# Moving x's split halves and the mixers' outputs by 32 bytes in a four-layer decoder on one Trainium2 core

## The reference

```python
for i in range(DEPTH):                      # DEPTH = 4
    mixer = i % 3
    h = rmsnorm(x, norm_mix[i])
    if mixer == 0:
        y = hgrn2_mixer(h, a_w_in[j], lower_bounds[j], a_head_norm[j], a_w_out[j])
    elif mixer == 1:
        y = moba_mixer(h, b_w_qkv[j], b_w_out[j], rel_bias)
    else:
        y = pool_mixer(h, c_w_group[j], c_scale[j])
    x = x + y
    x = x + sqrelu_mlp(rmsnorm(x, norm_mlp[i]), mlp_w1[i], mlp_w2[i])
return rmsnorm(x, norm_final)

def sqrelu_mlp(h, w1, w2):
    a = jax.nn.relu(h @ w1)
    return (a * a) @ w2
```

## Time and profile before

| | |
|---|---|
| median of the runs | 1209.92 us |
| the profiled execution | 1210.43 us |
| its span, first to last instruction | 1208.4 us |
| PE busy | 1176.4 us (97%), 6883 matmul records |
| PEld (weight loads) busy | 1039.2 us (86%) |
| DVE busy | 785.3 us (65%) |
| ACT busy | 672.7 us (56%) |
| granted TensorE clock, mean | 0.993 of full speed |

### The profile page before, as it was taken

The page is one execution under the profiler, slowest core; times in us unless marked ns, Lnnn a source line. Parts: engine busy times, 40 slices in busy tenths (PEclk is TensorE's granted clock), DMA queues, the critical chain, the costliest instruction groups (busy, mean ns, idle before and its releaser), DMA issues.

```text
span 1208.4 us, 17224 instructions
## 1 busy us (share of the span) xinstructions
PE 1176.4 (97%) x6883; PEld 1039.2 (86%) x6883; DVE 785.3 (65%) x794; ACT 672.7 (56%) x793; POOL 58.6 (5%) x36
## 2 busy tenths in 40 slices
PE   6999999999999999999999899999999999999998
PEld 5999998888889989888887788888888999888886
DVE  6678776655657555656655776656688777655663
ACT  5956675544545444544555654555687567544553
POOL 2000012000001003000000300000000001100000
PEclk8999999999999999999999999999999999999999
DMA  9543335654456435454644554645444333555450
GB/s 339 171 140 102 108 105 174 218 199 173 174 212 210 140 105 180 165 213 157 218 180 140 184 200 161 217 177 197 151 140 140 105 105 106 174 210 208 155 209 35
DMA packets 84856, 202.38 MB, mean 167 GB/s; under 512 B 3277, under 2 KB 5399, under 8 KB 84544
## 3 DMA queue, kind: packets, MB, share of 16 engines
q1 hardware_dynamic: 84768, 201.58, 48.0%
q0 software_dynamic: 32, 0.02, 0.0%
HBM read 200.52 MB, written 1.06 MB: 167 GB/s over the span
## 4 chain that ended last, share of the span: by engine, by line
PE 82%; DVE 7%; ACT 5%; POOL 3%; issue 2%; DMA 0%; SPq 0%; POOLq 0%; ACTq 0%; DVEq 0%
PE acc L631 9%; PE acc L632 9%; PE acc L633 9%; PE hb L584 8%; PE misc L584 7%; PE hb L589 4%; PE misc L589 4%; PE hb L533 3%; PE hb L532 3%; PE hb L530 3%; DVE wlo L1368 3%; POOL hn L1905 3%; PE acc L735 2%; ACT whi L990 2%; PE hb L547 2%; PE hb L545 2%
## 5 line engine op out<-in xcount | busy, mean ns | idle before, releaser
L1368 DVE TENSOR_TENSOR wlo<-raw,whi 128x2048 fp32r<-128x2048 f32 x186 | 421.1, 2293 | 163.4 <-ACT whi L990 163.4
L990 ACT ACTIVATE whi<-raw 128x2048 fp32r<-128x2048 f32 x186 | 348.3, 1906 | 113.0 <-PE acc L633 99.2
L631 PE MATMUL acc<-whi,arena_r 128*128 128x512 f32 x512 | 199.9, 390 | 0.0
L632 PE MATMUL acc<-wlo,arena_r 128*128 128x512 f32 x512 | 199.5, 390 | 0.0
L633 PE MATMUL acc<-whi,arena_r 128*128 128x512 f32 x512 | 199.2, 389 | 0.0
L584 PE MATMUL hb<-xhl,whi 128*128 128x512 f32 x512 | 128.3, 392 | 2.3 <-DVE arena L1804 2.3
L584 PE MATMUL misc<-xhl,whi 128*128 128x512 f32 x512 | 129.1, 393 | 1.4 <-DVE wlo L1368 1.4
L633 PEld LDWEIGHTS acc<-whi,arena_r 128*128 128x128 f32 x512 | 96.1, 188 | 20.2
L631 PEld LDWEIGHTS acc<-whi,arena_r 128*128 128x128 f32 x512 | 96.3, 188 | 19.1
L632 PEld LDWEIGHTS acc<-wlo,arena_r 128*128 128x128 f32 x512 | 96.2, 188 | 18.8
L584 PEld LDWEIGHTS misc<-xhl,whi 128*128 128x128 f32 x512 | 93.5, 188 | 20.4 <-DVE wlo L1368 2.6
(11 more groups left out here) (254 smaller groups left out, 1847.8 us busy)
## 6 DMA issues: line engine op xcount, KB each, us to landing
raw<-in_mlp_w_dram SPq DMA_DIRECT2D x128, 1024.0 KB, 5.4
raw<-in_a_w_in_dram SPq DMA_DIRECT2D x32, 1024.0 KB, 5.4
raw<-in_b_w_qkv_dram SPq DMA_DIRECT2D x12, 1024.0 KB, 7.1
raw<-in_a_w_out_dram SPq DMA_DIRECT2D x8, 1024.0 KB, 5.1
raw<-in_b_w_out_dram SPq DMA_DIRECT2D x4, 1024.0 KB, 5.1
arena<-in_x_dram SPq DMA_DIRECT2D x1, 1024.0 KB, 5.2
arena<-in_decay_dram SPq DMA_DIRECT2D x1, 1024.0 KB, 12.1
arena<-bias_rows SPq DMA_DIRECT2D x1, 1024.0 KB, 6.8
```

The costliest lines, as they stand in the source:

```text
L631: pe.matmul(o, ys, h, start=first and kt == 0, stop=False, skip_group_check=True)
L632: pe.matmul(o, ys, l, start=False, stop=False, skip_group_check=True)
L990: act.activation(whi[:, g % 2, u, 0:n], raw[:, g % 2, u, 0:n], ACT.Copy).then_inc(hi_done, 1)
L1368: dve.tensor_tensor(wlo[:, g % 2, u, 0:n], raw[:, g % 2, u, 0:n], whi[:, g % 2, u, 0:n].bitcast(F32), ALU.subtract).then_inc(lo_done, 1)
```

## The change

`xhl` gets 8 words (32 bytes) ahead of its data and 8 behind, and `oh` and `ol` begin 8 words into `arena_r`, which gets 16 words more. `yh` and `yl` keep their place and layout; they are only written without `oh` and `ol`, from which they used to be derived. `hh`, `hl`, `lfh`, `lfl`, `bh` and `bl` still begin at the start of `arena_r`. No instruction is added, removed or reordered on any engine; below the third changed line all line numbers grow by one (L631 becomes L632).

```diff
-        xhl = sb("xhl", [P, KT, 2, SEQ], F32R)
+        xhl_at = sb("xhl", [P, 8 + KT * 2 * SEQ + 8], F32R)
+        xhl = xhl_at[:, 8:8 + KT * 2 * SEQ].rearrange("p (a b c) -> p a b c", a=KT, b=2)
         xh, xl = xhl[:, :, 0, :], xhl[:, :, 1, :]
         arena = sb("arena", [P, 12800])
-        arena_r = sb("arena_r", [P, 4096], F32R)
+        arena_r = sb("arena_r", [P, 4096 + 16], F32R)
...
-        oh = arena_r[:, 0:2048].rearrange("p (a b) -> p a b", a=HEADS)
-        ol = arena_r[:, 2048:4096].rearrange("p (a b) -> p a b", a=HEADS)
+        oh = arena_r[:, 8:8 + 2048].rearrange("p (a b) -> p a b", a=HEADS)
+        ol = arena_r[:, 8 + 2048:8 + 4096].rearrange("p (a b) -> p a b", a=HEADS)
...
-        yh, yl = (w.rearrange("p (t a) b -> p t (a b)", t=TT) for w in (oh, ol))
+        yh, yl = (arena_r[:, at:at + 2048].rearrange("p (t a) -> p t a", t=TT) for at in (0, 2048))
```

## The result

The changed kernel takes 1218.64 us (median of four runs, 1218.19 to 1218.95), the kernel before 1210.08 us beside it: ratio 1.0073, 95% interval 1.0061 to 1.0086. It is slower by some 8.6 us, where a gain of 12.9 us was forecast. The time lies inside the stated range, in the case that had been given 25%.

What follows compares the result with a forecast made beforehand. TensorE's steps were taken to bound the kernel. Gains of 13.5 us in shifted matmuls and 0.6 us lost in `decay` sum to -12.9 us, so 1197 us from the median 1209.92, range 1163 to 1228 us.

Steps and rivals of the forecast that it cites:

- What bounds the kernel: Whole kernel: TensorE, busy 1176.4 of 1208.4 us, sets the time; matmul gains or losses pass on nearly one for one.
- Some 11 ns of each step: Split products: some 11 ns of each 227 ns step lost to stream and weight load interfering, depending on where operands lie.
- the mark: 512-column matmuls: lower bound of a step, taken from L479's float32 records, 216 ns instead of 227, worth 33 us.
- All that moves was counted: 5888 matmuls change distance: 3200 to +32, 576 to +96, 528 to -32, 1584 to -64 (`mlp_down` and the band).
- The value of the nearest row: All 5888 shifted matmuls: each gains the `decay` products' 2.3 ns at all four distances, 13.5 us less.
- an upper bound: All shifted matmuls: 512-column steps stay at the worst seen, 235 ns, and 256-column ones grow by 8 ns, +47 us.
- Rival 3: Products with x: the loss grows, 512-column steps of 235 instead of 227 ns become steady, +11.3 us, 1221 us; chance 25%.
- Rival 2: Whole kernel: nothing changes, as distance may matter only in larger steps; 1207.5 to 1212.3 us; chance 18%.
- The Trainium skill's rule: TensorE: separate ports for stream and weight load, so no placement could matter and time would stay at 1210 us.
- The count of 16-byte lines: SBUF: a 32-byte shift crosses as many 16-byte lines as before, so by that count nothing would change.
- ScalarE and VectorE at no cost: Accesses to shifted `xhl`, `oh`, `ol`: costed at nothing, 0 to +3 us kept; 499 and 519 ns should stay.

Runs made afterwards that it cites:

- the 64 bytes alone: Kernel before with only `hh` and `hl` moved 64 bytes into a longer `arena_r`: 1218.06 us against 1209.70, ratio 1.0074.
- the sweep: Decoder left out, only float32r matmuls at varied operand distances: 512 columns step 226.7 ns at 0, 233.3 at 192; 256 columns 120.0 and 113.3.
- the 32 bytes alone: Changed kernel with 512 bytes of padding, so only `xhl`, `oh` and `ol` shift, by 32: 1209.79 us against 1209.70 for the kernel before, ratio 1.0001.

## Why the prediction was wrong

- *What bounds the kernel* was right. TensorE's steps make the time: 48 steps per chunk at 233 in place of 227 ns came out in the time as 8.4 us of some 9.5 (the 64 bytes alone).
- *Some 11 ns of each step are an interference of stream and weight load, and it depends on where they lie.* The dependence is right: the sweep shows it with no other engine at work, with the two operands' distance as the only variable. That the whole 11 ns are such an interference is not shown. No distance gave 512 columns less than 226.6 ns, and the 215 ns that served as the mark are of unsplit float32; no run streams float32r without a load beside it.
- *All that moves was counted, `mlp_down` at -64 among it.* Right, and this count led to the cause.
- *The value of the nearest row stands for all four distances.* This step failed. The row was a 256-column product at +320 (which is 64), and it was used for 512-column products at -64. The 2.3 ns were right for the 256-column ones at +32 in sign and nearly in size (1.7 for L589, 2.4 for x's `t_block`); those at +96 gained nothing. For the 512-column ones the true term is +6.1 ns in `mlp_down`, +3.7 in L584, +4.1 in `w_half`: 15 us more in place of 7 less. The same distance of -64 that gives 256 columns their best step, 113.3, gives 512 columns 233.3. Both stand in the changed kernel: the band products, 256 columns at the same -64, went from 120 to 113.3 ns.
- *The trace held a hint.* In the earlier trace rows the 512-column steps off the steady 226.7 are longer, up to 235, and never shorter. They were taken at distance 0 and so measured no other distance, but they are of the right form, and they were used only for the rival and as an upper bound. For 512 columns the kernel before already stood at the least of the 26 distances (modulo 256) tried; of the others only 112 equals it.
- *Rival 3* had the mechanism: steps of 235 become the steady ones. It placed them on x's products and let `mlp_down` give back 3.6 us. x's products cancel among themselves (1209.79 us with the 32 bytes alone), and `mlp_down` is the loss (1218.06 us with the 64 bytes alone). That its 1221 us come near the 1218.64 is luck: x's 512-column products lost half of the 11.3 us taken for them, x's 256-column ones gave 4.5 back, and `mlp_down` cost 9.3.
- *Rival 2*, that 32 bytes may change nothing, is true of the sum of x's products and false of each term.
- *The Trainium skill's rule* of two independent read ports ("TensorE: Matmul & The Clock Gate", "Step-by-step: what each phase is for"), by which no placement could matter, does not hold here: the sweep's 226.7 to 234.1 ns for the same 512 columns, in steps of 32 bytes, differ by the operands' distance alone. The count of 16-byte lines ("SBUF — State Buffer", "Specifications (TRN2)") does not decide either: 32 bytes leave the count as it was and change the step by 6.6 ns.
- *ScalarE and VectorE at no cost* was right: 500 and 520 ns.

Open: by what in the stream's beginning the state of 113.3 or 117.8 ns is chosen, why 256 and 512 columns want different distances, and how own and next tile work together. Other operand types were not tried.

## What to carry to other kernels

In a kernel whose TensorE never waits, padding a buffer is a change to every matmul that reads what lies behind it: list the distance, modulo 256 bytes, between stream and stationary tile for each form before and after. A price seen on one width of the stream need not hold for another width, not even in its sign; take the nearest row of the same form, and ask on which side of it all the other values of that form lie. A pure stream of matmuls over the distances is one short run and would have settled the sign. When steps are compared between traces, leave out those at the lower clock.

## What the runs showed that was not expected

- The step of a float32r matmul with a weight load beside it ranges from 226.6 to 236.2 ns for 512 columns and from 113.3 to 120.1 ns for 256, by the operands' distance modulo 256 bytes in multiples of 16. Starts off a multiple of 16 gave up to 240.0 and 123.4 ns. The least is at 0 and 112 for 512 columns and at 192 for 256 (at 112 too, once settled).
- At the lower clock the one pair of distances on record shows no difference. Where the granted clock is 0.50 (1.2 GHz), the band products of 256 columns step by 213 ns both before, at distance 0, and after, at -64; at the 2.4 GHz level they have 120 and 113 ns. In the changed kernel, 9 matmuls from 669.90 to 671.82 and 15 from 674.17 to 675.87:

```profile
669.90 0.41 PE L951 MATMUL hb<-wlo,arena_r 128*128 128x256 f32 x1
...
671.82 0.41 PE L951 MATMUL hb<-wlo,arena_r 128*128 128x256 f32 x1
...
674.17 0.28 PE L951 MATMUL acc<-wlo,arena_r 128*128 128x256 f32 x1
...
675.87 0.28 PE L951 MATMUL acc<-wlo,arena_r 128*128 128x256 f32 x1
```

- The unsplit float32 products (L479, 215 ns for two passes of 256 columns) have the same step before and after.
- The same distance can have two steady states (113.3 and 117.8 ns at 64 and at 192).
- With distances that alternate, a step is not that of either tile: 231.6 ns where the distances alone give 226.7 on the one side, 228.9 and 233.3 on the other.
